# Attention projections: VectorE scales two blocks ahead of the next weight split, and the first two heads' transposes get two PSUM banks of their own

## What is computed

```python
c_kv = rms_norm(hk @ w_kv_a[:, :256], kv_a_norm_g)             # 512 x 256
kv = (c_kv @ w_kv_b).reshape(512, 16, 64 + 64)                 # k_nope and v of 16 heads
k_nope = rms_norm(kv[..., :64], k_nope_norm_g)                 # per token and head
q = (rms_norm(h @ w_dq, q_norm_g) @ w_uq).reshape(512, 16, 64 + 32)
q_nope = rms_norm(q[..., :64], q_nope_norm_g)
q_rope = apply_rope(rms_norm(q[..., 64:], q_rope_norm_g), cos, sin)
s = (q_nope @ k_nope.T + q_rope @ k_rope.T) / sqrt(96)         # per head
o = softmax(where(mask, s, -1e30)) @ v
```

## Time and profile before

| what | value |
|---|---|
| median of 3 runs | 2336.63 us (2336.56 to 2337.39) |
| the profiled execution | 2337.77 us, of which the span (first to last instruction) is 2336.0 |
| mean granted TensorE clock | 0.971 of full speed |
| the stage of the change | about 641 to 751 us of the span; the heads run from there to about 857 |

### The profile page before, as it was taken

How to read it: one execution, slowest core, us unless ns; L and a number is a source line. 1 busy time by engine, 2 the same in 40 slices (tenths; PEclk the granted TensorE clock), 3 DMA queues, 4 the chain that set the end, 5 groups by cost and what they waited for, 6 DMA issues and landing times.

```text
span 2336.0 us, 28735 instructions
## 1 busy us (share of the span) xinstructions
PE 2194.9 (94%) x10796; PEld 1709.1 (73%) x10796; DVE 1172.6 (50%) x1652; ACT 842.8 (36%) x1318; POOL 25.6 (1%) x29
## 2 busy tenths in 40 slices
PE   5779999999987899999999999999999998999998
PEld 3457687888765557888888777767888876888886
DVE  5886557575376665434334545555424344333333
ACT  5354432132254664423223444442222223222222
POOL 2100000000000000000000000000000000000000
PEclk8888999999998999999999999999999999999999
DMA  7635478676331004233233221222333322333332
GB/s 295 198 100 176 132 260 288 227 277 214 122 90 39 19 1 137 81 101 107 81 109 107 74 55 55 55 55 66 97 97 92 99 81 72 99 103 95 99 107 73
DMA packets 353035, 270.47 MB, mean 116 GB/s; under 512 B 12234, under 2 KB 338352, under 8 KB 342624
## 3 DMA queue, kind: packets, MB, share of 16 engines
q1 hardware_dynamic: 337144, 246.33, 34.2%
q10 hardware_dynamic: 15784, 22.69, 3.1%
HBM read 265.91 MB, written 3.08 MB: 115 GB/s over the span
## 4 chain that ended last, share of the span: by engine, by line
PE 82%; DVE 7%; ACT 3%; DVEq 2%; DMA 2%; issue 2%; ACTq 1%; SPq 0%; POOL 0%; POOLq 0%
PE G L543 60%; PE G L2143 9%; DMA hS<-in_ada_w 1%; DVE tb L623 1%; PE MS L2372 1%; PE X L2353 1%; PE X L2619 1%; DVE wlo L529 1%; ACT whi L523 1%; PE X L1885 1%; DVEq L622 1%; DMA TTall<-blocks 1%; PE X L1849 1%; PE X L2604 1%; DVE scan L782 1%
## 5 line engine op out<-in xcount | busy, mean ns | idle before, releaser
L529 DVE TENSOR_TENSOR wlo<-raw,whi 128x1024 fp32r<-128x1024 f32 (+1 forms) x296 | 380.7, 1287 | 801.1 <-ACT whi L523 797.5
L523 ACT ACTIVATE whi<-raw 128x1024 fp32r<-128x1024 f32 (+1 forms) x296 | 328.0, 1109 | 894.5 <-PE G L543 738.4
L543 PE MATMUL G<-Ahi,whi 128*128 128x512 f32 x1440 | 567.0, 394 | 17.4 <-DVE Alo L628 9.8
L543 PE MATMUL G<-Ahi,wlo 128*128 128x512 f32 x1440 | 562.7, 391 | 0.0
L543 PE MATMUL G<-Alo,whi 128*128 128x512 f32 x1440 | 562.3, 390 | 0.0
L543 PEld LDWEIGHTS G<-Ahi,whi 128*128 128x128 f32 x1440 | 271.5, 189 | 89.4 <-issue 19.9
L543 PEld LDWEIGHTS G<-Alo,whi 128*128 128x128 f32 x1440 | 271.6, 189 | 57.2
L543 PEld LDWEIGHTS G<-Ahi,wlo 128*128 128x128 f32 x1440 | 271.8, 189 | 55.0
L543 PE MATMUL G<-mhi,whi 128*128 128x512 f32 x528 | 206.9, 392 | 0.3 <-issue 0.3
L543 PE MATMUL G<-mlo,whi 128*128 128x512 f32 x528 | 205.6, 389 | 0.0
L543 PE MATMUL G<-mhi,wlo 128*128 128x512 f32 x528 | 205.5, 389 | 0.0
(11 more groups left out here) (556 smaller groups left out, 2625.4 us busy)
## 6 DMA issues: line engine op xcount, KB each, us to landing
raw<-in_w_in SPq DMA_DIRECT2D x64, 512.0 KB, 4.0
ada_ff<-in_w_ada SPq DMA_DIRECT2D x24, 1024.0 KB, 6.7
ada_ff<-in_ada_w SPq DMA_DIRECT2D x24, 1024.0 KB, 8.0
raw<-in_ffn_w_gate SPq DMA_DIRECT2D x44, 512.0 KB, 4.0
raw<-in_ffn_w_up SPq DMA_DIRECT2D x44, 512.0 KB, 4.0
raw<-in_ffn_w_down SPq DMA_DIRECT2D x32, 704.0 KB, 4.7
raw<-in_w_ffn_in SPq DMA_DIRECT2D x44, 512.0 KB, 3.9
ada_s<-in_ada_w SPq DMA_DIRECT2D x16, 1024.0 KB, 8.1
```

What stands on the lines that cost most here:

```text
L523: last = E.eng.activation(whi[j][:, k0:k0 + k, 0:c], raw[j][:, k0:k0 + k, 0:c], ACT.Copy)
L529: last = E.eng.tensor_tensor(wlo[j][:, k0:k0 + k, 0:c], raw[j][:, k0:k0 + k, 0:c], whi[j][:, k0:k0 + k, 0:c].bitcast(FP32), ALU.subtract)
L543: mm = E.eng.matmul(out_, a[j][:, k0 + kk, 0:c], b(kk), start=first and kk == 0 and n == 0, stop=last and kk == k - 1 and n == 2)
```

## The change

Three things. In `latent_act`, `c_squares` moves from slot 4 to slot 1. In `up_dve` the round of tile n becomes: scale 0 and scale 1 of tile n-1, split of tile n+1, sum 0, scale 2, sum 1, scale 3, sum 2, sum 3, merge. In the heads, the turns of heads 0 and 1 use bank X2 for queries and X3 for keys. The first turns then wait for `up_free` 29 (tile 6 is scaled, its X banks are free) in place of 33, the wait for 33 moves to `scores(0)`, and `copy_q(0)` and `copy_q(1)` move in between the scalings of tile 7.

```diff
@@ latent_act
             norm_act(E, col(mod[1], 0), lambda k: Bhi[:, k, :],
                      between={2: lambda: high_part(E, "kva", 2, 0), 3: lambda: high_part(E, "kva", 3, 1),
-                              4: c_squares, 7: kr_copy})
+                              1: c_squares, 7: kr_copy})
@@ up_dve
             for n in range(8):
+                if n > 0:
+                    scale(n - 1, 0)
+                    scale(n - 1, 1)
+                    if n < 7:
+                        low_part(E, "up", n + 1, (n + 1) % 2)
                 for b in range(4):
                     sums(n, b)
-                    if n > 0:
-                        scale(n - 1, b)
+                    if n > 0 and b < 2:
+                        scale(n - 1, b + 2)
                     if n == 0 and b == 1:
                         latent_root(E, [G[0][:, :], G[1][:, :]], V_QN)
                         v.sem_inc(S("up_free"), 1)
                 merge(n)
                 if n == 0:
                     latent_low(E, cqhi, cqlo)
-                if n < 6:
-                    low_part(E, "up", n + 2, n % 2)
                 if n == 5:
                     rotate_q(E, 0)
-            for b in range(4):
-                scale(7, b)
+            copy_q(E, 0)
+            scale(7, 0)
+            scale(7, 1)
+            copy_q(E, 1)
+            scale(7, 2)
+            scale(7, 3)
             v.drain()
@@ heads
+        QBANK = [X[2]] * 2 + [G[0]] * (NH - 2)
+        KBANK = [X[3]] * 2 + [G[0]] * (NH - 2)
...
             def turn_q(h):
                 E.eng.wait_ge(S("q_rotated"), h // 4 + 1)
-                if h > 0:
+                if h == 1:
+                    E.eng.wait_ge(S("tq_taken"), 1)
+                elif h > 1:
                     E.eng.wait_ge(S("tk_taken"), h)
...
             def turn_k(h):
-                E.eng.wait_ge(S("tq_taken"), h + 1)
+                if h == 1:
+                    E.eng.wait_ge(S("tk_taken"), 1)
+                elif h > 1:
+                    E.eng.wait_ge(S("tq_taken"), h + 1)
...
             def scores(h):
                 s = h % 2
                 E.eng.wait_ge(S("tk_taken"), h + 1)
+                if h < 2:
+                    E.eng.wait_ge(S("tq_taken"), h + 1)
                 if h > 0:
                     E.eng.wait_ge(S("exp_done"), h)
...
-            E.eng.wait_ge(S("up_free"), 33)
+            E.eng.wait_ge(S("up_free"), 29)
             E.eng.wait_ge(S("kr_act"), 6)
             for h in range(2):
                 turn_q(h)
                 turn_k(h)
+            E.eng.wait_ge(S("up_free"), 33)
             scores(0)
```

More of the change, by code:

```diff
@@ L2328, in program, with copy_q @@
         TBANK = (X[2][:, :], X[3][:, 0:384], AD[:, 0:256], X[3][:, 384:512])
+        QBANK = [X[2]] * 2 + [G[0]] * (NH - 2)
+        KBANK = [X[3]] * 2 + [G[0]] * (NH - 2)
+        def copy_q(E, h):
+            E.eng.wait_ge(S("tq_done"), h + 1)
+            E.eng.tensor_scalar(Q100[h % 2][0:QW, :], QBANK[h][0:QW, :], gq[:, 0:1], None, ALU.mult)\
+                .then_inc(S("tq_taken"), 1)
         def heads_pe(E):
@@ L2334, in turn_q @@
                 E.eng.wait_ge(S("q_rotated"), h // 4 + 1)
-                if h > 0:
+                if h == 1:
+                    E.eng.wait_ge(S("tq_taken"), 1)
+                elif h > 1:
                     E.eng.wait_ge(S("tk_taken"), h)
                 for b in range(4):
-                    mm = p.transpose(G[0][0:QW, b * P:(b + 1) * P], Qtok[:, b, h, :], ident)
+                    mm = p.transpose(QBANK[h][0:QW, b * P:(b + 1) * P], Qtok[:, b, h, :], ident)
                 mm.then_inc(S("tq_done"), 1)
             def turn_k(h):
-                E.eng.wait_ge(S("tq_taken"), h + 1)
+                if h == 1:
+                    E.eng.wait_ge(S("tk_taken"), 1)
+                elif h > 1:
+                    E.eng.wait_ge(S("tq_taken"), h + 1)
                 for b in range(4):
-                    mm = p.transpose(G[0][0:NST, b * P:(b + 1) * P], Ktok[:, b, h, :], ident)
+                    mm = p.transpose(KBANK[h][0:NST, b * P:(b + 1) * P], Ktok[:, b, h, :], ident)
                 mm.then_inc(S("tk_done"), 1)
@@ L2399, in copy_k @@
                 E.eng.wait_ge(S("tk_done"), h + 1)
-                a.activation(K100[h % 2][0:NST, :], G[0][0:NST, :], ACT.Copy).then_inc(S("tk_taken"), 1)
+                a.activation(K100[h % 2][0:NST, :], KBANK[h][0:NST, :], ACT.Copy).then_inc(S("tk_taken"), 1)
             def expo(h):
@@ L2437, in heads_dve @@
             v = E.eng
-            def copy_q(h):
-                E.eng.wait_ge(S("tq_done"), h + 1)
-                v.tensor_scalar(Q100[h % 2][0:QW, :], G[0][0:QW, :], gq[:, 0:1], None, ALU.mult)\
-                    .then_inc(S("tq_taken"), 1)
             def maxi(h):
@@ L2468, in low @@
                     v.drain().then_inc(S("part_ready"), 1)
-            copy_q(0)
-            copy_q(1)
             maxi(0)
@@ L2478, in heads_dve @@
                 if h + 2 < NH:
-                    copy_q(h + 2)
+                    copy_q(E, h + 2)
                 if h > 0:
```

## The result

| | before | changed |
|---|---|---|
| median of the comparison | 2336.60 us (2335.82 to 2337.39, 4 executions) | 2322.91 us (2321.30 to 2324.53, 4 executions) |
| ratio | | 0.9939, 95% interval 0.9927 to 0.9951 |
| profiled span, mean granted clock | 2336.0 us, 0.971 | 2321.7 us, 0.975 |

The change gained 13.7 us by the medians, 14.3 by the ratio; forecast were 10.3. The sign and the three mechanisms were as forecast, the size was not.

What follows compares the result with a forecast made beforehand. The prediction took matmuls to pace the rounds up to tile 4, VectorE and ScalarE from tile 5. Its terms, 0.6 + 4.3 + 5.4 = 10.3 us off the median of 2336.63, gave 2326.3 us, range 2322.7 to 2329.6.

Steps and rivals of the forecast that it cites:

- What bounds the stage: Latents to first scores: matmuls pace the rounds up to tile 4, VectorE and ScalarE from tile 5 on.
- Term 1: Latents: squares in slot 1 end before TensorE needs them, removing its 2.52 us wait; 0.6 us gained, bounds 0 and 1.0.
- Term 2: Tile rounds: two scales and the rotation move into VectorE's idle time before the split; 4.3 us, bounds 3.3 and 4.6.
- Term 3: First turns: run beside VectorE's last sums, scores 3.8 us after the last roots for 9.24; 5.4 us, bounds 4.4 and 6.
- is what I can't work out: TensorE's clock around tile 7 and the turns: short bursts between three waits may find either level; no amount in the sum.
- warm: Turns keep TensorE at full clock into the first scores and heads: 2 to 4 us more gain, 2323.3 us; chance 0.15.
- cold: Clock falls in the gap before tile 7 and stays, slowing tile 7, turns and heads: gain 7.1, 2329.2 us; chance 0.13.
- The range: Whole program: 2322.7 to 2329.6 us, covering the forecast's own case and most of warm and cold, leaving about 2 in 10 out.

Runs made afterwards that it cites:

- after_c: The changed kernel run again with no edit, a further set of executions: median 2326.24 us, ratio 0.9951.
- after_d: The changed kernel run a fourth time with no edit: median 2321.86 us, ratio 0.9931.
- fill_both: The changed kernel plus unread transposes on TensorE in the latents' wait and around the first turns: 2319.55 us (0.9922), again 2318.48 (0.9918).
- turns_only: The kernel before with only the first two heads' turns in X2 and X3 and their copies between tile 7's scales: 2332.69 us (0.9977).
- turns_b: turns_only measured again, against the kernel before: 2331.36 us (0.9973).

## Why the prediction was right and wrong

- **What bounds the stage.** Right. TensorE's waits in the query tiles and at the turns were the chain's, and taking them away shortened the program.
- **Term 1**, 0.6: measured 0.59 (20.98 to 20.39, means of two and four profiles). Right.
- **Term 2**, 4.3: 4.32 from the second half of tile 1 to the root of tile 7 (741.62 - 697.94 = 43.68 against 736.79 - 697.43 = 39.36), each round within 0.05. Right.
- **Term 3**, 5.4: 9.24 became 3.78, so 5.46, and 5.9 where the turns had full clock (`after_c` and `after_d`, 3.4). Right.
- **The sum's missing term.** The step that failed is the one that says the clock "is what I can't work out": it put the clock's effect at zero in the middle and left it to two rivals of nearly equal chance and opposite sign. It was not symmetric. In the pair of profiles of the first comparison, 3.9 of the 14.25 us lie in the stretches that no term covers, 1.57 in tiles 0 and 1 and 2.30 in the heads. Over all profiles of the two kernels it is less. Between the first and the last mark the kernel before took 215.0 us (mean of two profiles) and the changed one 202.2 (mean of four), 12.8 less. The first and third stretches bring 0.59 + 9.87 = 10.5, the terms of the prediction. The second brings 1.58 and the heads 0.76, 2.3 us in stretches whose work is the same and whose length went with the clock in all 17 profiles. The 1.58 is well borne out by the seven and eight profiles of the two slots. The 0.76 is not: it is the difference of two and four profiles, and the two of the kernel before are 1.7 apart. Of the 90 and 19 executions' difference of 13.15, 0.3 is left and lies inside its uncertainty. That shorter waits let the clock fall less often is how I read the counts; why a given wait brings a fall in one execution and none in the next stays open.
- **The rival "warm"** was right in its sign, at some 0.8 us on average in the heads, not 2 to 4, and that little is not settled: in the four profiles of the changed kernel the clock still fell at the turns or the first scores (heads at 0.96). It missed the place where more was won, tiles 0 and 1, where the clock was in no term at all. The fall was there to be read in the profile before: a mean clock of 0.65 from 684 to 688, behind the wait of 2.66 us that follows the transposes of the earlier trace rows. That moving the squares would change the odds of a stretch at half clock I had not seen.
- **The rival "cold"** had a rule of the Trainium skill beside it, "TensorE: Matmul & The Clock Gate", section "A second HAM failure mode: psum-queue depth-cycling", by which small gaps cost throughput as the clock goes up and down. That going up and down costs time this case shows: the heads took 117.62 us at 1.00 (`fill_both`) and 121.48 at 0.96. That the shorter gaps would win less than the idle time they remove came out the other way, 12.8 us for the terms' 10.5. What "cold" feared did happen in `after_c`, tile 7 at half clock, but it cost 0.4 us (39.78 for 39.36) and not the 1 us in the rival's sum. Counted from the forecast, that rival's own time should also have been 2329.5, not 2329.2.
- **The range.** It was drawn around a shift of 10.3 from the bounds of the terms. The pooled shift of 13.15, taken from the prediction's base of 2336.63, gives 2323.5 and lies in it, as the pooled mean of 2324.55 does. That the first comparison fell at its edge is partly luck: its four executions of the changed kernel lie 1.6 us below the mean of all 19. The range did not reckon with the spread of single executions, some 10 us for either kernel; the three executions shown before, within 0.8 us, made the kernel look steadier than it is.

Open: why sets of the same kernel differ (2327.9 in one, 2321.9 in another), and what decides whether a wait brings a fall of the clock. The parts of the program before the first mark took 656.4 to 661.2 us in the changed kernel's four profiles, and the parts after the last mark 1459.6 to 1463.0, with identical instructions; I did not follow these up.

## What to carry to other kernels

Put work that needs only an early result ahead of the wait for a later one on an in-order engine: two scales and a rotation moved into idle time were worth 4.3 us with not one instruction less. When waits of TensorE are shortened, look at its clock as well as at the wait, in the stages behind it too, and check it by filling the waits with matmuls that nobody reads. Here the fillings at the turns brought another 3.5 us between the marks, all of it in the heads. And where single executions spread by more than the effect, compare the times between marks in the profiles, which in the latents and in tiles 0 and 1 repeated to under 0.1 us at equal clock, and pool the executions before believing a median.

## What the runs showed of the hardware

TensorE's granted clock moved between its two levels (2.4 and 1.2 GHz, 1.00 and 0.50 in the rows) at different places in different executions of one program. In one kernel (`turns_only` and `turns_b`) the latents took the 1.5 us of a stretch at half clock in one profile, and tiles 0 and 1 in the other. The falls that I followed came in or shortly behind a wait of TensorE: 2.52 us ahead of the sums of squares, 2.66 ahead of tile 0, 2.40 and 1.23 ahead of the first and the third turn. A wait alone did not bring a fall: the 2.66 us ahead of tile 0 stood in all 14 profiles that don't fill it, and in 7 of them the clock fell. The work of the 16 heads took 117.6 us at 1.00 and 123.8 at 0.94. Extra matmuls made the kernel faster. The Trainium skill, "TensorE: Matmul & The Clock Gate", section "HAM oscillation — how this bites in real kernels", advises, for a matmul with few rows, to order the loop so that TensorE works through its tiles in one go before it waits for a DMA, and so stays warm. The waits here are for other engines and not for DMA, but the two profiles of `fill_both` agree with its aim: heads at 1.00 in 117.6 us.
